# The first stage of a two-layer fp32 kernel: half of the modulation columns as plain fp32 products, token high parts by ScalarE, loads in a new order

## What is computed

```python
m_l = (silu(c) @ w_ada + b_ada)[:, None, :]      # w_ada: 1024 x 6144
m_c = silu(c_ctx) @ w_ada + b_ada
sh1, sc1, g1, sh2, sc2, g2 = split(m_l, 6)
hl = rmsnorm(lat, norm_g[0]) * (1 + sc1) + sh1    # latent tokens
hc = rmsnorm(cx, norm_g[0]) * (1 + csc1) + csh1   # context tokens
q, zf_fwd, zf_bwd, v, g = split(h @ w_in, 5)      # w_in: 1024 x 5120
```

## Time and profile before

| | |
|---|---|
| median of three runs | 923.89 us (923.06 to 924.14) |
| the profiled execution | 925.75 us, its span 923.9 us |
| PE busy | 900.8 us (97%), 6320 instructions |
| PEld (weight loads) busy | 824.7 us (89%) |
| DVE busy | 662.3 us (72%) |
| ACT busy | 500.0 us (54%) |
| mean granted TensorE clock | 0.994 |
| products of `values` (L1198) end | 92.27 us |

### The profile page before, as it was taken

How to read it: one execution, slowest core, us unless ns; L and a number is a source line. 1 busy time by engine, 2 the same in 40 slices (tenths; PEclk the granted TensorE clock), 3 DMA queues, 4 the chain that set the end, 5 groups by cost and what they waited for, 6 DMA issues and landing times.

```text
span 923.9 us, 17154 instructions
## 1 busy us (share of the span) xinstructions
PE 900.8 (97%) x6320; PEld 824.7 (89%) x6320; DVE 662.3 (72%) x1099; ACT 500.0 (54%) x776; POOL 0.2 (0%) x4
## 2 busy tenths in 40 slices
PE   6899999999999999999999999999999999999997
PEld 5368888888899999999999899999999899999996
DVE  5878488888888676676677988886566766555555
ACT  6742366666665565555556654444464564444443
POOL 0000000000000000000000000000000000000000
PEclk9899999999999999999999999999999999999999
DMA  8829563333435266556555543345446456555551
GB/s 327 343 92 337 217 219 125 131 133 129 125 115 171 81 206 197 176 175 199 172 174 163 189 151 136 135 142 181 160 158 206 139 172 216 182 182 185 188 187 54
DMA packets 45343, 160.94 MB, mean 174 GB/s; under 512 B 5104, under 2 KB 6512, under 8 KB 45168
## 3 DMA queue, kind: packets, MB, share of 16 engines
q1 hardware_dynamic: 43536, 156.56, 49.7%
q10 hardware_dynamic: 1760, 3.74, 1.1%
HBM read 159.23 MB, written 1.05 MB: 173 GB/s over the span
## 4 chain that ended last, share of the span: by engine, by line
PE 89%; DVE 4%; ACT 2%; DMA 1%; issue 1%; SPq 1%; DVEq 0%; ACTq 0%
PE bank L454 21%; PE bank L456 21%; PE bank L455 21%; PE bank L1198 4%; PE bank L520 4%; PE bank L521 4%; PE bank L522 4%; DMA arena<-in_stream 1%; DVE w_lo L448 1%; PE bank L1259 1%; PE bank L1301 1%; PE bank L1281 1%; PE bank L1297 1%; PE bank L1231 1%; ACT w_hi L437 1%
## 5 line engine op out<-in xcount | busy, mean ns | idle before, releaser
L448 DVE TENSOR_TENSOR w_lo<-raw,w_hi 128x1024 fp32r<-128x1024 f32 x248 | 299.6, 1222 | 127.7 <-ACT w_hi L437 127.4
L454 PE MATMUL bank<-h_hi,w_hi 128*128 128x256 f32 (+1 forms) x1232 | 368.9, 299 | 2.1 <-DVE w_lo L448 1.1
L456 PE MATMUL bank<-h_hi,w_lo 128*128 128x256 f32 (+1 forms) x1232 | 362.0, 294 | 0.0
L455 PE MATMUL bank<-h_lo,w_hi 128*128 128x256 f32 (+1 forms) x1232 | 361.4, 293 | 0.0
L437 ACT ACTIVATE w_hi<-raw 128x1024 fp32r<-128x1024 f32 x248 | 257.2, 1051 | 112.7 <-PE bank L456 85.7
L454 PEld LDWEIGHTS bank<-h_hi,w_hi 128*128 128x128 f32 x1232 | 231.6, 188 | 12.4 <-issue 2.9
L455 PEld LDWEIGHTS bank<-h_lo,w_hi 128*128 128x128 f32 x1232 | 232.9, 189 | 6.4
L456 PEld LDWEIGHTS bank<-h_hi,w_lo 128*128 128x128 f32 x1232 | 231.5, 188 | 5.8
L454 PE MATMUL bank<-y_hi,w_hi 128*128 128x256 f32 x304 | 86.8, 286 | 0.0
L456 PE MATMUL bank<-y_hi,w_lo 128*128 128x256 f32 x304 | 85.8, 282 | 0.0
L455 PE MATMUL bank<-y_lo,w_hi 128*128 128x256 f32 x304 | 85.4, 281 | 0.0
(11 more groups left out here) (258 smaller groups left out, 1154.1 us busy)
## 6 DMA issues: line engine op xcount, KB each, us to landing
raw<-in_stream SPq DMA_DIRECT2D x248, 512.0 KB, 3.4
arena<-in_ada SPq DMA_DIRECT2D x24, 512.0 KB, 5.3
arena<-in_stream SPq DMA_DIRECT2D x6, 1024.0 KB, 14.4
xres<-in_ada SPq DMA_DIRECT2D x8, 512.0 KB, 3.3
tok<-in_tok SPq DMA_DIRECT2D x4, 512.0 KB, 10.3
con<-in_con ACTq DMA_DIRECT2D x1, 1472.0 KB, 9.6
xres<-in_tok ACTq DMA_DIRECT2D x1, 1024.0 KB, 9.1
out<-arena SPq DMA_DIRECT2D x4, 256.0 KB, 2.0
```

What stands on the lines that cost most here:

```text
L448: dve.tensor_tensor(w_lo[c.slot][:, :], source(c), w_hi[c.slot][:, :].bitcast(F32), ALU.subtract).then_inc(S("split_lo"), 1)
L454: pe.matmul(dst, hi_w, a_hi, start=start, stop=False, skip_group_check=True)
L455: pe.matmul(dst, hi_w, a_lo, start=False, stop=False, skip_group_check=True)
L456: return pe.matmul(dst, lo_w, a_hi, start=False, stop=stop, skip_group_check=True)
```

## The change

The sixteen modulation chunks are cut another way: a quarter q now holds shift and scale of tiles 2q and 2q+1. Quarters 0 and 1 are not split. Their eight chunks lie in `ada_raw`, and `ada_columns` multiplies them as plain fp32: the weight values are the stationary 128 x 128, silu(c) and silu(c_ctx) are two moving columns, and the result comes out as columns, with no copy and no turn. Quarters 2 and 3 are split and multiplied as before, through the ring. Value chunk 0 comes ahead of the ring's first modulation chunk, value chunk 1 between the two split quarters; the second quarter of plain columns is done after the third token block of `values(0)`. ScalarE makes the high parts of the tokens: for tiles 0, 1, 5, 6 (`DIRECT`) straight from the normalised tokens, while VectorE computes the same value again in `wide` for the low part; for the other tiles by a second pass, a copy. The loads come in the order of use, and warm-up products are moved (`WARM` 40, `FILL` 12). `load_mods` is spread otherwise, and `mod_tiles(0)` and `(1)` stand earlier on VectorE.

```diff
-N_HEAD = ADA_FIRST + KT
+N_HEAD = 2 * KT
-WARM = 12
-TOPPED = (5, 5, 5, 4, 0, 0, 0, 0, 0, 6)
+WARM = 40
+FILL = 12
+MODS_BEHIND = (9, 12, 13, 14, 15, 16)
+DIRECT = (0, 1, 5, 6)
-TURN_BANKS = (6, 7, 4, 5)
+TURN_BANKS = {2: 4, 3: 5}
+def split_number(i):
+    return i - KT + (1 if i < KT + 4 else 2)
 def value_number(j):
-    return V_FIRST if j == 0 else 2 * KT + j
+    return 5 * j if j < 2 else KT + j
...
+            load_tokens(0)
+            load_tokens(1)
+            load_tokens(2)
+            load_ada(0)
+            load_tokens(3)
+            load_ada(1)
+            load_ada(2)
+            load_one(0)
             sp.dma_start(par[:, :], par_in).then_inc(S("par_in"), 16)
+            for i in range(3, KT):
+                load_ada(i)
+            for n in range(1, RING + 1):
+                load_one(n)
...
             load_mods(0)
             load_mods(1)
+            for n in range(RING + 1, N_HEAD + AHEAD):
+                load_one(n)
+                if n in MODS_BEHIND:
+                    load_mods(2 + MODS_BEHIND.index(n))
...
                 for at, gain, shift in ((k * TC, gain_l, mod), (k * TC + T, gain_c, mod_c)):
                     x = tok[:, at:at + T]
-                    act.activation(x, x, ACT.Identity, scale=..., bias=...).then_inc(S("modulated"), 1)
+                    if k in DIRECT:
+                        act.activation(h_hi[:, at:at + T], x, ACT.Identity, scale=..., bias=...).then_inc(S("h_hi"), 1)
+                    else:
+                        last = act.activation(x, x, ACT.Identity, scale=..., bias=...)
+                if k in DIRECT:
+                    return
+                last.then_inc(S("modulated"), 1)
+                act.wait_ge(S("modulated"), ...)
+                act.activation(h_hi[:, x], tok[:, x], ACT.Copy).then_inc(S("h_hi"), 2)
...
+            def ada_columns(q):
+                for i in range(4 * q, 4 * q + 4):
+                    pe.wait_ge(S(f"ada_in{i}"), 16)
+                    for b in range(2):
+                        k = 2 * (i % 4) + b
+                        for m in range(4):
+                            last = pe.matmul(psum[4 + q][:, 2 * m:2 * m + 2], ada_raw[i][:, (4 * b + m) * P:(4 * b + m + 1) * P],
+                                             cs_pairs[:, k, :], start=k == 0 and m == 0, stop=k == KT - 1, skip_group_check=True)
+                    if i == 1:
+                        pe.wait_ge(S("tok_added"), KT - 1)
+                        pe.matmul(psum[1][:, :], ones, wide[:, 0:TC], start=True, stop=True).then_inc(S("tok_summed"), 1)
+                last.then_inc(S("ada_summed"), 1)
...
             def values(j, between=None):
-                    pe.wait_ge(S("h_lo"), 2 * k + 2)
...
+                        pe.wait_ge(S("h_hi"), 2 * k + 1 + tile // 2)
+                        pe.matmul(dst, h_hi[:, x], hi_w, start=k == 0, stop=False, skip_group_check=True)
+                        pe.matmul(dst, h_hi[:, x], lo_w, start=False, stop=False, skip_group_check=True)
+                        pe.wait_ge(S("h_lo"), 2 * k + 2)
+                        last = pe.matmul(dst, h_lo[:, x], hi_w, start=False, stop=k == KT - 1, skip_group_check=True)
...
+                        if b == 0 and tile == 2 and between is not None:
+                            between()
...
+            ada_columns(0)
+            warm(FILL)
+            values(0, lambda: ada_columns(1))
+            ada_rows(2)
+            values(1, lambda: turn_rows(2))
+            ada_rows(3)
+            values(2, lambda: turn_rows(3))
+            for j in range(3, KT):
                 values(j)
...
+            def low_tokens(k):
                 x = slice(k * TC, (k + 1) * TC)
+                src = tok
+                if k in DIRECT:
+                    src = wide
+                    dve.wait_ge(S("mod_first"), k // 2 + 1)
+                    dve.wait_ge(S("tok_normed"), k + 1)
...
+                        last = dve.tensor_scalar(wide[:, at:at + T], tok[:, at:at + T], gain[:, k:k + 1], shift[:, k:k + 1], ALU.mult,
+                                                 ALU.add)
...
                 dve.wait_ge(S("h_hi"), 2 * k + 2)
+                dve.tensor_tensor(h_lo[:, x], src[:, x], h_hi[:, x].bitcast(F32), ALU.subtract).then_inc(S("h_lo"), 2)
...
+            for k in range(2, 6):
+                lo(dve, Chunk(10 + k))
                 mod_tiles(k)
             move_odd(1)
+            for k in range(6, KT):
+                lo(dve, Chunk(N_HEAD, k - 6))
                 mod_tiles(k)
```

More of the change, by code:

```diff
@@ L1166, in _, with ada_rows @@
             pe.wait_ge(S("con_in"), 16)
[L1168 to L1178, removed]
+            def ada_columns(q):
[10 more added lines that the diff above has]
+                last.then_inc(S("ada_summed"), 1)
+            def ada_rows(q):
+                for i in range(4 * q, 4 * q + 4):
+                    c = Chunk(split_number(i))
+                    pe.wait_ge(S("split_lo"), c.n + 1)
+                    for b in range(2):
+                        k = 2 * (i % 4) + b
+                        for part_ in (w_hi, w_lo):
+                            last = pe.matmul(psum[4 + q][0:4, :], cs_w[:, 4 * k:4 * k + 4], part_[c.slot][:, b * 512:b * 512 + 512],
+                                             start=k == 0 and part_ is w_hi, stop=k == KT - 1 and part_ is w_lo,
+                                             skip_group_check=True)
+                    last.then_inc(S("multiplied"), 1)
             def turn_rows(q):
-                pe.wait_ge(S("mod_rows"), q + 1)
+                pe.wait_ge(S("mod_rows"), q - 1)
                 for m in range(4):
@@ L1193, in values @@
                     k = 2 * (j % 4) + b
-                    pe.wait_ge(S("h_lo"), 2 * k + 2)
                     for tile in range(4):
                         x = slice(k * TC + tile * P, k * TC + (tile + 1) * P)
[L1197 to L1200, removed]
+                        dst = psum[4 * half + tile][:, :]
@@ L1622, in quarter @@
-                dve.wait_ge(S("scale_first"), q + 2)
-                for gain, scale in ((gain_l, mod), (gain_c, mod_c)):
-                    dve.scalar_tensor_tensor(gain[:, tiles], scale[:, x], 1.0, p1("norm1", 4 * (q // 2), 4), ALU.add, ALU.mult)
+                tiles, split = slice(2 * q, 2 * q + 2), q in TURN_BANKS
+                before = 2 * q + (2 * (q - 2) if split else 0)
+                if split:
+                    dve.wait_ge(S("mod_turned"), q - 1)
+                    turned = psum[TURN_BANKS[q]][:, 0:16].rearrange("p (s k w) -> p s k w", s=2, w=4)
+                else:
+                    dve.wait_ge(S("ada_summed"), q + 1)
+                    turned = psum[4 + q][:, 0:8].rearrange("p (s k w) -> p s k w", s=2, w=2)
@@ L1626, in norm_tokens @@
+                done = before + (4 if split else 2)
+                for w, gain, scale in ((0, gain_l, mod), (1, gain_c, mod_c)):
+                    dve.wait_ge(S("quarter_part"), done - 1 + w)
+                    last = dve.scalar_tensor_tensor(gain[:, tiles], scale[:, KT + 2 * q:KT + 2 * q + 2], 1.0, p1("norm1", 2 * q, 2),
+                                                    ALU.add, ALU.mult)
+                last.then_inc(S("mod_first"), 1)
             def norm_tokens(k):
```

244 lines of the change are left out of this document (90 added, 154 removed).

## The result

The changed kernel takes 929.08 us (median of 6 runs, 928.88 to 932.61) beside 923.85 us for the kernel before (6 runs, 923.06 to 925.42): ratio 1.0061, 95% interval [1.0045, 1.0078]. The medians lie 5.2 us apart: the changed kernel is slower, where 6.5 us less was forecast. The profiled execution took 929.37 us, its span 927.6 us.

A forecast was written before the change was run, and what follows sets the result against it. TensorE was taken as the bound, with gain only before 92.3 us: values ending at 83.8 instead of 92.27 give -8.5, plus 2 for handovers, -6.5, so median 917.4 us from 923.89; range 914.8 to 926.5.

The forecast's parts named there:

- Plain columns: First two column quarters: 64 passes at 0.107 us make 6.85 us each, 13.7 for both, +6.2 us of TensorE work.
- the rival: Clock falls during plain columns, 15.1 us at most, about half if late: 928 (924 to 932); slower 22%, mostly this.
- the weighing: Whether 6.9 us of narrow column work counts as busy for TensorE's clock gate; taken as yes, so the sum stays.
- the 2 us added for handovers: Added back for four slack-free handovers in the middle and five under 1 us in the tail; between 0 and about 5.
- Loads: First 28 us: landing times in the new order, third token piece 10.6 us, plain chunk 0 11.9, first value chunk 17.0.
- The wait that the fill hides: Before `values(0)`: 24 fill passes (2.6 us) end at 23.1; without them TensorE's wait would be 2.4 us.
- The middle: Split quarters and `values(1)` to `values(3)`, 35.6 to 61.1 us: chunks just in time, four slack-free handovers.
- the row: Profile row: a load issued at 66.40 behind two of `load_mods` released ScalarE at 72.30, 5.9 us.
- The tail: `values(4)` to `values(7)`: 22.7 us, ending at 83.8 instead of 92.27, -8.5; slack under 1 us at chunks 13 to 17.
- The rival of the tail: Ring loads queued behind the sums lose 1 to 1.5 us at chunks 13, 15, 17: 921; with one clock fall, 14%.
- Carried one for one: Everything behind 92 us follows TensorE, so the whole gain reaches the end: -6.5 us.
- No wait of TensorE over 1 us behind the first chunks: Listed among the signs that would show the forecast right, at the first plain chunks.

The follow-up runs named there:

- the padded kernel: Changed kernel with each plain column product's moving side widened to 128 columns, of which the last two are real: 919.4 us, ratio 0.9939.

## Why the prediction was wrong

The direction was wrong by one step; of the rest, only one load in the middle came in later than the working had it. The step is in "Plain columns": "I take 0.107, as TensorE was warmed up to the first of them; the other end is a rival below". The first 32 passes did take 0.109, then the clock fell and they took 0.209. In terms of the sum, the +6.2 us for the columns was right only for the full clock, and it had nothing for the sum of squares, the fill and the value products that ran at the half clock behind them.

The price of that is 9.9 us on the end of the values and 9.7 on the time (929.1 against 919.4; 10.4 when each is set against the kernel before in its own series, 923.9 and 924.6), inside the bounds given for the rival (about half of 15.1, to 15.1). Its parts, from the starts in the two listings of TensorE above, the changed kernel against the padded one:

| | forecast, at most | measured |
|---|---|---|
| first quarter of columns | 4.4 | 3.1 |
| sum of squares | 1 | 0.95 |
| fill | 2.2 | 2.5 |
| second quarter | 5.9 | 2.15 |
| value products behind it | 1.6 | 2.6 |

The second spell began 4.7 us into its quarter, so most of those passes still ran at full clock; the price per pass was 0.209 us, a little over the 0.199 taken. Together these are 11.3 us; 0.7 us is given back further on, where the padded kernel waits for load 10, and another 0.7 lies in its later start of the columns. The rival's own time, 928 from 924 to 932, is what came out; it was given most of a 22% chance. The measured 929.08 lies above the stated range, 914.8 to 926.5.

What misled was the weighing. The Trainium skill ("TensorE: Matmul & The Clock Gate", Part 1) says that the gate follows how busy the engine has been, and I let that stand for the narrow columns. The traces say otherwise: busy 4.00 of 4.00 us, granted 0.50. The same page's remark on transposes (Part 4), that they do not count as busy in the same way, describes what the narrow columns did, though no run here tests transposes; I named it and gave it too little. The evidence offered by my rows, bursts of 1.7 us that left the clock alone, could not carry a forecast for 6.9 us; in the changed kernel the clock, too, was still full 3.5 us into the columns.

The other steps, checked on the padded kernel, in which the clock holds:

- End of the values: 83.8 by the sum and 85.8 with the 2 us added for handovers; measured 86.13. Time: -6.5 forecast; measured -5.2 between the medians, -5.6 by the ratio 0.9939. That the sum came so close is in part luck, as the 2 us were a round figure for nine handovers and one late load took most of them.
- Loads: 1.8 us too late in my table. The third token piece released ScalarE at 8.78 us in the changed kernel (10.6 forecast), the value chunk at 15.20 (17.0). It gained nothing, since plain chunk 0 came after the warm-up anyway.
- First product of `values(0)`: 23.1 forecast, 23.5 measured. The wait that the fill hides: 2.4 forecast, 1.84 measured without it.
- The middle: `values(2)` was to start at 49.3 and started at 51.76, of which 1.5 us was waiting. The sum took load 10 to be there in time; it took 6.3 us, from 43.09 to 49.39, behind two transfers of `load_mods`. This is the row again, which I applied to the tail and not here.
- The tail: low half 13 was ready at 67.9 us (65.8 to 66.6 forecast), about 1.2 us before its use; chunk 15 11.6 us after it (11.2 forecast), still 1 us before its use. The rival of the tail cost nothing.
- Carried one for one: the values end 6.1 us earlier than before, the span is 6.2 us shorter.
- "No wait of TensorE over 1 us behind the first chunks" came true in the changed kernel too and showed nothing: with the products at the half clock the other engines are in time (longest wait 0.8 us).

## What to carry to other kernels

A plain fp32 product with a full set of weights and few moving columns (2 or 32 here) keeps TensorE busy in the profile and lets its clock fall. If a pass takes no longer with more columns (0.109 us with two, 0.112 with 128), widen the moving side with zeros, and read the granted clock beside every busy share. When the waits on the bounding engine vanish and the time does not, look at the duration of one instruction first. A load's place in its queue counts: with two transfers of 512 KB ahead of it, load 10 released ScalarE 6.3 us after its issue, and 1.5 us of waiting went when they were moved behind it.

## What the runs showed that was not expected

- Plain 128x128 products in a row: at 128 and at 64 moving columns the granted clock stayed at full (2.4 GHz), at 32 and at 2 it fell to half (1.2 GHz), all at 0.109 to 0.112 us a pass while the clock was full (with 32 columns some of the ten runs were faster, so the fall there may be partial).
- Wide passes in between, 1.2 us after every 1.7 us of narrow ones, delayed the fall by some 6 us and did not prevent it.
- In the block of narrow products put in by itself the clock fell about 2.5 us in, stayed at the half to its end at 94 us and some 4 us into the dense value products behind it, so 64 such products cost 27.3 us where the wide ones cost 13.8.
- The granted clock reads 1.00 from the start of the kernel, yet the first warm-up passes last 0.421 us each, as those at granted 0.50 do, and the later ones 0.275. Where this changes differs from run to run (about 4 us in one profile, over 6 in another), and so the columns begin anywhere from 11.65 to 12.91 us in kernels that are the same up to there. In the first microseconds the duration of a pass tells more than the reading.
